# A causal convolution spread over eleven beats with a second accumulator, and decay arguments split from their scan

## The reference

```python
def gdn_mixer(qkv_raw, z, a_raw, b_raw, conv_w, ...):
    qkv = jax.nn.silu(causal_depthwise_conv(qkv_raw, conv_w))   # 4 taps
    q, k, v = split(qkv)
    qc, kc = l2norm(q) * DK ** -0.5, l2norm(k)
    ...
def gla_mixer(q, k, v, r, g_lr, ...):
    cum = jnp.cumsum(log_alpha)          # within a chunk
    q_dec = q * jnp.exp(cum); k_inv = k * jnp.exp(-cum)
    scores = causal(q_dec @ k_inv.T)
    ...
```

## Time and profile before

| | before |
|---|---|
| runs, median (lowest to highest) | 2795.93 us (2795.72 to 2798.47) |
| profiled execution | 2795.09 us |
| its span, first to last instruction | 2793.0 us |
| busy TensorE | 2667.6 us (96%) |
| busy VectorE | 1900.2 us (68%) |
| busy ScalarE | 993.3 us (36%) |
| busy GpSimd | 496.5 us (18%) |
| mean granted TensorE clock | 0.982 of full |

### The profile page before, as it was taken

How to read it: one execution, slowest core, us unless ns; L and a number is a source line. 1 busy time by engine, 2 the same in 40 slices (tenths; PEclk the granted TensorE clock), 3 DMA queues, 4 the chain that set the end, 5 groups by cost and what they waited for, 6 DMA issues and landing times.

```text
span 2793.0 us, 44953 instructions
## 1 busy us (share of the span) xinstructions
PE 2667.6 (96%) x16632; PEld 2349.2 (84%) x16632; DVE 1900.2 (68%) x3625; ACT 993.3 (36%) x2228; POOL 496.5 (18%) x433
## 2 busy tenths in 40 slices
PE   7999999999999999999999999998999999999998
PEld 3789889888988988998998898897978888888887
DVE  4667767867877776776776776776566666666656
ACT  4633553473364355336326335432430000000002
POOL 0000310220140031000000000000044344333341
PEclk9999999999999999999999999999999999999999
DMA  6221121112112112212212212323112111111111
GB/s 203 61 57 31 35 65 47 31 50 56 28 49 71 30 31 63 56 31 53 62 28 59 57 28 50 76 59 120 33 61 61 46 46 53 53 46 46 46 46 61
DMA packets 222618, 152.44 MB, mean 55 GB/s; under 512 B 27856, under 2 KB 207032, under 8 KB 222400
## 3 DMA queue, kind: packets, MB, share of 16 engines
q1 hardware_dynamic: 209728, 141.70, 17.3%
q0 software_dynamic: 12672, 7.87, 2.9%
HBM read 133.28 MB, written 16.26 MB: 54 GB/s over the span
## 4 chain that ended last, share of the span: by engine, by line
PE 68%; DVE 20%; ACT 10%; issue 2%; DMA 1%; SPq 0%; DVEq 0%; ACTq 0%
PE bank L179 26%; PE bank L171 17%; PE bank L2067 8%; DVE sig L1048 2%; PE bank L968 2%; PE bank L1194 2%; DVE feat_region L1619 2%; PE bank L1186 2%; DVE wB_lo L1101 1%; DVE feat_region L1623 1%; DVE wA_lo L1101 1%; PE bank L443 1%; PE bank L1141 1%; PE bank L1128 1%; ACT conv_in L1655 1%
## 5 line engine op out<-in xcount | busy, mean ns | idle before, releaser
L171 PE MATMUL bank<-wB_hi,h_hi 128*128 128x256 f32 x1024 | 298.9, 292 | 12.7 <-ACT rows_region L1012 10.7
L171 PE MATMUL bank<-wA_hi,h_hi 128*128 128x256 f32 x1024 | 299.4, 292 | 11.5 <-ACT rows_region L1012 9.4
L171 PE MATMUL bank<-wA_lo,h_hi 128*128 128x256 f32 x1024 | 299.2, 292 | 0.0
L171 PE MATMUL bank<-wA_hi,h_lo 128*128 128x256 f32 x1024 | 298.7, 292 | 0.0
L171 PE MATMUL bank<-wB_lo,h_hi 128*128 128x256 f32 x1024 | 298.5, 292 | 0.0
L171 PE MATMUL bank<-wB_hi,h_lo 128*128 128x256 f32 x1024 | 298.1, 291 | 0.0
L179 PE MATMUL bank<-h_hi,wA_hi 128*128 128x512 f32 x672 | 270.3, 402 | 2.7 <-DVE feat_region L981 2.2
L179 PE MATMUL bank<-h_hi,wA_lo 128*128 128x512 f32 x672 | 269.4, 401 | 0.0
L179 PE MATMUL bank<-h_hi,wB_hi 128*128 128x512 f32 x672 | 269.2, 401 | 0.0
L179 PE MATMUL bank<-h_lo,wA_hi 128*128 128x512 f32 x672 | 268.8, 400 | 0.0
L179 PE MATMUL bank<-h_hi,wB_lo 128*128 128x512 f32 x672 | 268.3, 399 | 0.0
(11 more groups left out here) (390 smaller groups left out, 6134.7 us busy)
## 6 DMA issues: line engine op xcount, KB each, us to landing
w_raw<-in_w_in_dram SPq DMA_DIRECT2D x96, 512.0 KB, 3.7
w_raw<-in_w_ffn_up_dram SPq DMA_DIRECT2D x44, 512.0 KB, 3.7
rows_region<-in_ada_w_dram SPq DMA_DIRECT2D x64, 256.0 KB, 2.6
w_raw<-in_w_ffn_down_dram SPq DMA_DIRECT2D x22, 512.0 KB, 3.5
rows_region<-in_x_dram SPq DMA_DIRECT2D x8, 512.0 KB, 7.9
w_raw<-in_w_in_dram SPq DMA_DIRECT2D x16, 256.0 KB, 2.9
y_scratch<-ybuf SPq DMA_DIRECT2D x32, 128.0 KB, 1.9
y_scratch<-ybuf POOLq DMA_DIRECT2D x32, 128.0 KB, 3.1
```

The costliest lines, as they stand in the source:

```text
L171: mm = nc.tensor.matmul(bank[:, n_out:n_out + n1 - n0], (h_hi, h_lo)[hp][:, k, t * P:t * P + P], buf[wp][:, k, n0:n1], start=(s == 0), sto ...
```

## The change

A convolution now takes one tap a beat and ends later: VectorE's taps in offsets 1, 2 and 3, ScalarE's absolute value and exponential in 5, logarithm in 6, VectorE's log-sigmoid step in 8, ScalarE's exponential in 9, VectorE's product in 10, the square in 12 and the norm sums in 14. k has an accumulator of its own: `pair_buf[:, 0:S]`, which the delta rule does not use in that stretch, and in the lead-in `kt_sub[:, 0]`. So k no longer waits for q's product, the starts no longer keep nine beats of distance (10, 18 and 27 for i >= 0; 9, 17 and 26 in the lead-in), and v waits only for q's product. The gates start in beat 33. In the lead-in the first load of `mod_sp` waits for k's product instead of an earlier event. `prep_dve` gets two stages: scan, edges and `gla_cum` in beat 5c - 8 as before, the two argument instructions in beat 5c - 7.

```diff
                 elif i == 0:
-                    sp.wait_ge(sem("xt_up"), 2 * KT)
+                    sp.wait_ge(sem("conv_silu"), 2)
...
-    def prep_dve(dve, step, i, c):
+    def prep_dve(dve, step, i, c, stage):
...
+        if stage == 1:
+            for half in range(2):
+                n = 64 * (half + 1)
+                step(dve.tensor_tensor(kt_sub[:, c % 2, 4 * half:4 * half + 4, 0:n],
+                                       edges[:, 4 * half:4 * half + 4].unsqueeze(2).broadcast_to([P, 4, n]),
+                                       cum[:, 0:n].unsqueeze(1).broadcast_to([P, 4, n]), ALU.subtract), "gla_arg")
+            return
...
         q, k, v = (unit_done[GDN[i] + 2 * j + 1] - p2(i) + 2 for j in range(3))
-        k = max(k, q + 9)
-        CONV_AT[i] = (q, k, max(v, k + 9))
-    GATES_AT = {i: CONV_AT[i][1] + 13 for i in GDN}
+        CONV_AT[i] = (q, k, v)
+        assert k >= q + 4 and v >= max(k + 4, q + 13)
+    SQ, SS = 12, 14
+    GATES_AT = {i: CONV_AT[i][1] + SS + 1 for i in GDN}
+
+    def acc_of(i, j):
+        if j == 1:
+            return kt_sub[:, 0].rearrange("p m n -> p (m n)") if i < 0 else pair_buf[:, 0:S]
+        return conv_acc
...
-            if o in (1, 2):
-                for tap in ((1, 2), (3,))[o - 1]:
-                    if tap == 1:
-                        dve.wait_ge(sem("conv_tap"), 3 * (i + 1) + j + 1)
+            acc = acc_of(i, j)
+            if 1 <= o < GDN_TAPS:
+                if o == 1:
+                    dve.wait_ge(sem("conv_tap"), 3 * (i + 1) + j + 1)
+                if j < 2:
+                    step(dve.scalar_tensor_tensor(acc, conv_in[:, j % 2, o:o + S], conv_w[:, o, j:j + 1], acc, ALU.mult,
+                                                  ALU.add), "conv" if o == GDN_TAPS - 1 else None)
...
-            elif o == 6:
+            elif o == 8:
                 dve.wait_ge(sem("conv_e"), 3 * (i + 1) + j + 1)
...
-            elif o == 8:
+            elif o == 10:
                 dve.wait_ge(sem("conv_sig"), 3 * (i + 1) + j + 1)
...
                 if j == 0:
                     act.wait_ge(sem("conv_w"), i + 2)
-                else:
-                    act.wait_ge(sem("conv_silu"), 2 * (i + 1) + j)
+                elif j == 2:
+                    act.wait_ge(sem("conv_silu"), 2 * (i + 1) + 1)
...
-            elif o == 3:
+            elif o == 5:
...
-            elif o == 4:
+            elif o == 6:
...
-            elif o == 7:
+            elif o == 9:
...
-            elif o == 9 and j < 2:
+            elif o == SQ and j < 2:
...
-            if r == CONV_AT[i][j] + 12:
+            if r == CONV_AT[i][j] + SS:
...
-                at_ = chunk_at(b, PREP_DVE)
-                if at_ and branch(at_[0]) == "gla":
-                    prep_dve(dve, step, *at_)
+                for stage in range(2):
+                    at_ = chunk_at(b, PREP_DVE + stage)
+                    if at_ and branch(at_[0]) == "gla":
+                        prep_dve(dve, step, *at_, stage)
```

More of the change, by code:

```diff
@@ L1437, in prep_dve @@
                                edges[:, 0:NT].unsqueeze(2).broadcast_to([P, NT, SUB]), ALU.subtract), "gla_cum")
-        for half in range(2):
-            n = 64 * (half + 1)
-            step(dve.tensor_tensor(kt_sub[:, c % 2, 4 * half:4 * half + 4, 0:n],
-                                   edges[:, 4 * half:4 * half + 4].unsqueeze(2).broadcast_to([P, 4, n]),
-                                   cum[:, 0:n].unsqueeze(1).broadcast_to([P, 4, n]), ALU.subtract), "gla_arg")
     def prep_pool(pool, step, i, c):
@@ L1613, in conv_dve @@
             e = conv_in[:, j % 2, GDN_TAPS - 1:]
-            if o in (1, 2):
-                for tap in ((1, 2), (3,))[o - 1]:
-                    if tap == 1:
-                        dve.wait_ge(sem("conv_tap"), 3 * (i + 1) + j + 1)
-                    if j < 2:
-                        step(dve.scalar_tensor_tensor(conv_acc[:], conv_in[:, j % 2, tap:tap + S],
-                                                      conv_w[:, tap, j:j + 1], conv_acc[:], ALU.mult, ALU.add),
-                             "conv" if tap == GDN_TAPS - 1 else None)
-                    else:
-                        step(dve.scalar_tensor_tensor(conv_acc[:, tap:], v_t[:, 0:S - tap],
-                                                      conv_w[:, GDN_TAPS - 1 - tap, j:j + 1], conv_acc[:, tap:],
-                                                      ALU.mult, ALU.add),
-                             "conv" if tap == GDN_TAPS - 1 else None)
-            elif o == 6:
+            acc = acc_of(i, j)
[5 more added lines that the diff above has]
+                                                  ALU.add), "conv" if o == GDN_TAPS - 1 else None)
+                else:
+                    step(dve.scalar_tensor_tensor(acc[:, o:], v_t[:, 0:S - o], conv_w[:, GDN_TAPS - 1 - o, j:j + 1],
+                                                  acc[:, o:], ALU.mult, ALU.add),
+                         "conv" if o == GDN_TAPS - 1 else None)
+            elif o == 8:
                 dve.wait_ge(sem("conv_e"), 3 * (i + 1) + j + 1)
-                step(dve.scalar_tensor_tensor(e, conv_acc[:], 0.0, e, ALU.min, ALU.subtract), "conv_ls")
-            elif o == 8:
+                step(dve.scalar_tensor_tensor(e, acc, 0.0, e, ALU.min, ALU.subtract), "conv_ls")
+            elif o == 10:
                 dve.wait_ge(sem("conv_sig"), 3 * (i + 1) + j + 1)
-                step(dve.tensor_tensor((kq[:, 1], kq[:, 0], v_t[:])[j], conv_acc[:], e, ALU.mult),
+                step(dve.tensor_tensor((kq[:, 1], kq[:, 0], v_t[:])[j], acc, e, ALU.mult),
                      "conv_silu" if j < 2 else "conv_v")
@@ L1654, in conv_act @@
                     act.wait_ge(sem("conv_ss"), 2 * (i + 1) + 1)
-                step(A(e, conv_acc[:], ACT.Abs))
+                step(A(e, acc, ACT.Abs))
                 step(A(e, e, ACT.Exp, scale=-1.0))
-            elif o == 4:
+            elif o == 6:
                 step(A(e, e, ACT.Ln, bias=1.0), "conv_e")
-            elif o == 7:
+            elif o == 9:
                 act.wait_ge(sem("conv_ls"), 3 * (i + 1) + j + 1)
                 step(A(e, e, ACT.Exp), "conv_sig")
-            elif o == 9 and j < 2:
+            elif o == SQ and j < 2:
                 act.wait_ge(sem("conv_silu"), 2 * (i + 1) + j + 1)
```

5 lines of the change are left out of this document (2 added, 3 removed).

## The result

The changed kernel takes 2776.1 us (median of 5 runs, 2773.6 to 2779.5) against 2795.9 for the kernel before: ratio 0.9933, 95% interval 0.9918 to 0.9949, about 19.8 us less. The forecast was 2769.5 with 2745 to 2793 around it; so the direction and most of the size came, and 6.6 us did not.

The account below looks back on a forecast made before the run. TensorE was mostly busy, but the VectorE and ScalarE ping-pong set the time in the convolution's window. 4 x 3.9 + 3 x 5.0 + 4.5 = 35 us, less 9 for the clock, net 26: 2769.5 us, range 2745 to 2793.

Parts of the forecast that it names:

- The walk of head 1: GLA head 1's part 2, new order at full clock: beat 34 at 603.9 instead of 607.8, gain 3.9 us a GLA head.
- The second buffer: Convolution: k's first tap no longer waits for q's product; counted within the 3.9 us a GLA head, without its own size.
- One tap a beat: Convolution: q's taps in beats 11, 12, 13; q's convolution still ends at 561.5, ScalarE gets the scan 1.3 us earlier.
- The arguments at nothing: Decay arguments a beat later in each chunk: costed at nothing; 1.15 us a chunk if GpSimd's cover were gone.
- The lead-in: Eviction moves ahead of v's absolute value: gain 3.4 us plus part of the slow stretch behind it, 4.5 us.
- The walk gave beat 34 of head 4: mLSTM head 4: beat 34 starts at 1298.8 instead of 1303.8, gain 5.0 us an mLSTM head.
- 7 x 1.3: Clock toll in the seven heads: half-clock stretches after short waits and one-column sums take back 9 us, at most 14.
- The full cover: Rival: the VectorE and ScalarE chain vanishes under TensorE, gain 60 us, time 2735; chance 0.12.
- The gain eaten: Rival: GpSimd meetings and half clock take 3 to 4 us a head: 2784 to 2791; gain 5.6 to 14 had chance 0.12.
- Slower by the queue head: Rival: q's exponential over 4 us late delays k's taps, scan and masks; at 5.5 us late, 2806; chance 0.08.
- Arguments that starve GpSimd: Rival: later arguments delay GpSimd's product and the scores, a 1.15 us wait in 4 heads: 2774; no separate chance given.
- More meetings of VectorE and GpSimd: Spread-out taps could meet GpSimd at 0.9 us each; two more a GLA head cost 7 us, leaving 19; no chance given.

Follow-up runs that it names:

- run 12: Kernel before, with only ScalarE's weight halves made behind the convolution's step: 2776.8 us, ratio 0.9925.
- experiment 3: Kernel before with k's own accumulator and the starts 10, 18, 27 alone, old offsets, taps and arguments: 2774.5 us, ratio 0.9926.
- experiment 1: Kernel before with only the decay arguments moved a beat after their scan: 2789.9 us, ratio 0.9970.
- experiment 2: Changed kernel with the arguments put back into their scan's beat: 2778.3 us, ratio 0.9938 to the kernel before.
- experiment 5: Changed kernel with sums of squares at offset 15 instead of 14, which also moves the gates a beat: 2763.8 us, ratio 0.9884 to the kernel before.
- experiment 4: Changed kernel with the later convolution's tap ahead of the earlier one's product on VectorE: 2775.1 us, ratio 0.9924 to the kernel before.
- experiment 6: Changed kernel with ScalarE's weight halves made behind the convolution's step: 2768.3 us, ratio 0.9897 to the kernel before.
- run 9: Changed kernel with sums of squares a beat later and ScalarE's weight halves behind the convolution's step: 2759.9 us, ratio 0.9866 to the kernel before.
- run 8: Kernel of experiment 3 with ScalarE's weight halves made behind the convolution's step: 2764.1 us, ratio 0.9882 to the kernel before.
- run 10: Kernel of experiment 3 with TensorE's sums of squares one beat later: 2774.9 us, ratio 0.9921 to the kernel before.
- experiment 7: Kernel of experiment 3 with TensorE's sums of squares two beats later: 2798.3 us, ratio 1.0002 to the kernel before.

## Why the prediction was right, and where it was off

**The bound** was read rightly: the ping-pong of VectorE and ScalarE, not TensorE, set the time of the convolution's beats. Moving two lines of ScalarE's order, with every matmul where it was, took 21 us (run 12).

**The walk of head 1** held step by step. With 10.47 us added: k's tap 1 ended 571.5 (walk 571.2), q's exponential 574.3 (574.2), the product 575.6 (575.5), the mask 578.0 (577.8), k's absolute value began 583.2 (582.9), the wide bank's eviction 588.6 (588.4), beat 34 at 604.3 (603.9). Gain 3.5 us, of which 0.36 had come by the end of part 1; 3.9 forecast. One step was missing: the output matmul waits for `ybuf` too, one instruction and 0.5 us behind the mask, so the wait was 1.65 us and not 0.9. TensorE reached the wide bank that much later, and waited 1.35 there, not 2.3.

**The second buffer** was the main term, and experiment 3 shows that it carries everything. **One tap a beat**, with the later offsets, was taken as part of the same gain; on top of the buffer it gives nothing measurable. It exchanged 19.9 us at the sums for 16.7 at the output matmul and 5.4 on L1005.

**The arguments at nothing** was wrong for the change done alone (0.3%, experiment 1) and right within the change as far as the medians tell (experiment 2). The walk had both orders of q's beats, but asked only whether the arguments come too late for their reader, not what their going frees in the queue.

**The lead-in** was 4.5 in the forecast and 5.7 measured.

**The clock is the mis-sized term, in the mLSTM heads above all.** The walk gave beat 34 of head 4 at 1298.8, 5.0 us before the old one. It came at 1283.53, which with the lead of 19.11 at the head's start is 1302.64: 1.2 us. The waits were as walked in sum though not one by one (3.38 and 0.57, together 3.95, against 2.2 and 1.7, together 3.9; L1012 0.44), so the waits are not what failed. Of the 3.8 us that are missing, 3.4 are the two stretches at half clock, behind q's sums and behind k's: the walk was made at full clock. What failed is "7 x 1.3" for the clock, an equal sum for each head. The half clock of the table above cost 15.4 us in the three mLSTM heads, where 3.9 were allowed, and they kept 1.2 us of the 11.1 net that they were given. In the four GLA heads it cost 6.8, where 5.2 were allowed, and they kept 10.5, which is 2.6 each on average (1.7 to 3.5; 2.6 was 3.9 less 1.3). The seven heads together: 30.6 gross less 22.2 for the clock is 8.4; 11.7 came. The 22 also lies above the prediction's upper bound of 14. Experiment 5 shows that most of this half clock belongs to where the one-column sums and the gates stand, not to the length of the wait: with q's wait unchanged, 20.5 us of half clock are left in the seven heads instead of 44.4.

**Against the kernel before, the clock gave and did not take.** TensorE's busy time did not rise by 9 us but fell by 6.9 (2.1 of them ahead of the lead-in's projection), and waits gave 14.5 of a span gain of 21.4. Both readings hold: the walk sets a new order at full clock beside the old one as it ran, with its own half clock (54.6 us in the seven heads, 27 us of cost), so its gross gain already counts getting rid of all of that. **Part of the hit is luck.** The clock took 13 us more than the 9 allowed, and the profiled span's gain of 21.4 missed the net 26 by only 4.6 (6.6 by the medians), because the seven heads gave 3.3 more ahead of the clock's toll than walked, the lead-in gave 1.2 more, and 4.0 us (2.9 ahead of the lead-in's projection, 1.1 at the end) lie where the sum had nothing.

**Rivals.** The full cover (2735) fell: no kernel here came near. The gain eaten (2784 to 2791) fell for the kernel but roughly holds for the mLSTM heads, where a sign named for a wrong forecast, more half clock than before, came true as well (23.9 to 30.7 us). Slower by the queue head fell: q's exponential came when the walk said. Its mechanism is real, though (VectorE idles 2.16 us with q's product at its head in head 1). Arguments that starve GpSimd: no such wait appeared. More meetings of VectorE and GpSimd, for which the Trainium skill was cited ("SBUF — State Buffer", section "SBUF: two separate sides"): six taps of head 1's part 2 took 8.0 us instead of 7.7, so the rule changed next to nothing in the changed kernel. In experiments 4, 6 and 9 q's product meets GpSimd in all four GLA heads and takes 1.69 to 2.00 us instead of 1.23 (experiment 6), up to 0.8 us a head of what those edits were to win.

```profile
L1628 DVE SCALAR_TENSOR_TENSOR feat_region<-conv_in,conv_w,feat_region 128x1024 f32<-128x1024 f32 x6 | 8.0, 1332 | 0.5 <-ACT feat_region L1656 0.4
```

## What to carry to other kernels

When two in-order queues hand work to and fro, look first at what stands in front of the late instruction within its own beat: putting ScalarE's weight halves behind the convolution's step gave as much in the old kernel as a second buffer and eleven new beats. Before crediting a removed wait, name the next thing that TensorE will ask for, and all that it waits for. Split a span into busy and idle time at an equal count of matmuls: it tells whether an edit won waits or clock, and an edit that shortens no main wait can win 12 us by moving small matmuls away from behind a wait. When an edit brings an instruction forward, look at what GpSimd does at its new time.

## What the runs showed of the hardware

- The same wait can cost very different times. In the changed kernel and in run 5 the output matmul of head 4 waits 3.38 us; with the sums right behind, the next 4.83 us are granted 0.65 of the clock (levels 2.4 and 1.2 GHz), with projection matmuls between, 1.00 is granted. It is no certainty: in head 5 of run 5, with the same wait and the same order as in head 4, 6.83 us are at half clock.
- Sixteen one-column sums directly behind a wait, even a short one, were followed by half clock nearly always: in the kernel before (waits of 1.59 us in the four GLA heads, 2.96 in the three mLSTM heads) and in runs 3, 8 and 10 in all seven heads, in runs 1 and 12 in six of seven, behind waits from 0.6 us on. With the six output matmuls (1.4 us) between a wait of 1.65 us and q's sums, none of the four GLA heads of the changed kernel or of run 2 shows it.
- Behind a wait of 4.25 to 4.30 us (experiment 7) all seven heads run at half clock for 3.4 to 13.7 us; in head 1 577.50 to 580.79 is granted 0.50, and sixteen single-column matmuls take 3.41 us instead of 1.84.
- Heads with equal waits differ by up to 2.5 us within one execution (231.8 to 234.3), by 0 to 6.83 us at half clock; in run 9, with no half clock in the four GLA heads, they agree to 0.7. Why a stretch is 3.4 us long in one head and 6.8 or 10.2 in the next, at the same order and the same wait, stays open: no run here isolates it.
- A VectorE product of two operands of 128 x 1024 that started 0.9 us before GpSimd's multiplication ended took 2.00 us instead of 1.23 (experiment 6).
